# Hybrid block with product-key experts: spreading the gates with one 256-column matmul per token

## The chip, the core and the metric

One core of a Trainium2 chip runs the whole program. The metric is the device time of one execution in microseconds (us), the median of several. Engines are called PE (TensorE), DVE (VectorE), ACT (ScalarE), POOL (GpSimd) and SP (SyncE, which here only issues DMAs).

## What is computed

The program is one layer of a hybrid encoder block on 1024 tokens of width 1024: RMSNorm, an input projection, a recurrent group and an attention group, an output projection, and then the product-key expert part (PEER), followed by a last RMSNorm. The change lies in the expert part, cut here to what matters:

```python
# h: 1024 tokens x 1024; experts: 128 x 128 = 16384 single neurons; 8 heads x 16 picks = 128 picks a token
experts = (e1 * 128 + e2).reshape(t, 128)
gates = jax.nn.softmax(top_s, axis=-1).reshape(t, 128)
pre = jnp.einsum('td,tkd->tk', xb, u_tab[eb])
act = jax.nn.gelu(pre) * gb
y = jnp.einsum('tk,tkd->td', act, v_tab[eb])
```

## The kernel before

The expert part has three functions: `score` (queries, scores and picks), `experts_up` (activations) and `experts_down` (the second table). The change touches only `experts_up`, lines 1114 to 1485.

`experts_up` handles the 1024 tokens in two ways. Three tiles of 128 tokens are handled **by rows**: for each token and pick POOL fetches the expert's row of `u` with an indirect DMA (`fetch`, L1349) and DVE takes its dot product with the token (`dot`, L1453), 384 dots in all. The other 640 tokens are handled **densely**: all 16384 activations are computed by PE, and the gates are spread over all 16384 experts, mostly as zeros, so that `experts_down` can multiply the two.

The dense products run over 128 chunks `c` of the table, each 128 experts x 1024. SP loads a chunk (`load`, L1213), ACT rounds it to the high part `uT_hi` (`high`, L1287), DVE subtracts to get the low part `uT_lo` (`low`, L1436; POOL does it for the first 24 chunks, L1340), PE multiplies in three terms, 24 matmuls of 320 columns for each half of the tokens (`multiply`, L1251), ACT applies the gelu (`gelu`, L1301), and SP stores the activations (L1221).

The gates are spread by one-hot vectors, 4 tokens at a time; the 640 tokens are 160 such groups `g`. For each token two 128 x 128 matrices are made: `first_hot` (which of the 128 first keys each pick has) and the one of the second key, scaled by the gate. To keep the precision of fp32 with matmuls in float32r, the gate is split into a high and a low part. DVE makes the one-hots of a group (`hot_group`, L1446 and L1447), ACT scales them into `second_hot_lo` and `second_hot_hi` (`gate`, L1309 and L1312), PE multiplies `first_hot` with the high and with the low part into the same PSUM columns (`spread_out`, two 128-column matmuls per token, L1241 and L1243), and ACT copies the 512 sums to SBUF, 32 tokens innermost (`spread_out` of ACT, L1294). This copy writes one element per 128 bytes:

```python
A(spread[:, part % 2, :, col * GROUP:(col + 1) * GROUP].rearrange("p e t -> p t e"),
  spread_ps[:, g % 2], ACT.Copy).then_inc(spread_read, 1)
```

Eight groups make a part of 32 tokens, 2 MB, which SP stores to DRAM (L1227), 20 parts in all.

The order of the work is written out by hand. Every engine goes through the same count `q` of quarters, four for each chunk, 512 in all, with 12 dense matmuls in each; its instructions stand in that order and it never turns back. `groups_at(q)` lists the groups that PE spreads and ACT copies in quarter `q`: 160 groups over the quarters 84 to 496, one in 2.575 quarters. DVE makes the one-hots of a group five quarters earlier, ACT scales them four quarters earlier, `low(c + 1)` stands at the second quarter of chunk `c` (DVE q = 4c + 1), `high(c + 1)` at its first (ACT q = 4c), and the dots are spread over the quarters 58 to 508. Seven steps that turn picks into keys (`key`, L1400 to L1409) come in for each of the eight tiles of tokens.

The waits that tie the engines: `high(c)` waits for its load and for PE to be done with chunk c - 2; `low(c)` waits for `high(c)`; PE starts chunk c after `low(c)`. SP's queue is in order too: load of chunk c + 2, store of the activations of chunk c (which waits for both gelus), then the store of a part of gates if its last group lies in that chunk (which waits for `spread_read`), then the next load. A load that follows a store of gates therefore stands behind it.

Of the kernel before, what the change touches and what calls it, by code (L numbers as in the profile page):

```python
# [1113 lines left out]
def experts_up(nc, d, m, sem):  # L1114
# [22 lines left out]
    KEY_STEPS, TURN_AFTER = 7, 12  # L1137

# [21 lines left out]
    with ExitStack() as own_memory:  # L1160
# [7 lines left out]
        second_hi = sb("second_hot_hi", [P, SLOTS, GROUP, NK], F32R)  # L1168
        second_lo = sb("second_hot_lo", [P, SLOTS, GROUP, NK], F32R)
# [9 lines left out]
        pre = ps("expert_pre", [P, 4, HALF])  # L1179
        spread_ps = ps("spread_ps", [P, 2, GROUP, NK])  # L1180
# [7 lines left out]
        spread_done, spread_read = sem("spread_done"), sem("spread_read")  # L1188
# [18 lines left out]
        with nc.Block() as block:  # L1207
# [27 lines left out]
            def _(pe):  # L1235
                def spread_out(g):
                    pe.wait_ge(gates_hot, g + 1)
                    if g >= 2:
                        pe.wait_ge(spread_read, g - 1)
                    for j in range(GROUP):  # L1240
                        nc.tensor.matmul(spread_ps[:, g % 2, j], first_hot[:, g % SLOTS, j],  # L1241
                                         second_hi[:, g % SLOTS, j], start=True, stop=False)
                        last = nc.tensor.matmul(spread_ps[:, g % 2, j], first_hot[:, g % SLOTS, j],  # L1243
                                                second_lo[:, g % SLOTS, j], start=False, stop=True)
                    last.then_inc(spread_done, 1)
# [3 lines left out]
                def multiply(c, half, n):  # L1249
                    part, t, k = terms[n]  # L1250
                    last = nc.tensor.matmul(pre[:, (2 * c + half) % 4, 0:WIDTH], part[:, c % 2, k],  # L1251
# [13 lines left out]
                for q in range(QUARTERS):  # L1265
# [3 lines left out]
                    if q % 2 == 0 and 2 * c + half >= 4:  # L1269
                        pe.wait_ge(act_done, 2 * c + half - 3)  # L1270
# [9 lines left out]
            def _(act):  # L1280
# [8 lines left out]
                def spread_out(g):  # L1289
                    part, col = divmod(g, PART)  # L1290
                    act.wait_ge(spread_done, g + 1)
                    if col == 0 and part >= 2:
                        act.wait_ge(spread_stored[part % 2], 16 * (part // 2))
                    A(spread[:, part % 2, :, col * GROUP:(col + 1) * GROUP].rearrange("p e t -> p t e"),  # L1294
                      spread_ps[:, g % 2], ACT.Copy).then_inc(spread_read, 1)

                def gelu(c, half):
                    act.wait_ge(pre_done, 2 * c + half + 1)
                    if half == 0 and c >= 2:
                        act.wait_ge(act_stored[c % 2], 16 * (c // 2))  # L1300
                    A(act_out[:, c % 2, half * WIDTH:(half + 1) * WIDTH], pre[:, (2 * c + half) % 4, 0:WIDTH],  # L1301
                      ACT.Gelu_apprx_tanh).then_inc(act_done, 1)
# [61 lines left out]
            def _(dve):  # L1364
# [84 lines left out]

                def dot(k):  # L1450
# [6 lines left out]
                for q in range(KEYS_FROM, QUARTERS + 4):  # L1457
# [11 lines left out]
                    for n in range(3):  # L1469
                        for t in tiles_at(q, TURN_AFTER + 2 + n):  # L1470
                            if t >= F:
                                keep(t, n)
                    for g in hots_at(q):
# [372 lines left out]
```

## Time and profile before

| | us |
|---|---|
| median of 3 runs | 3349.49 (3339.14 to 3357.92) |
| the profiled execution | 3346.13 |
| its span in the profile | 3344.3 |
| PE busy | 2998.9 (90% of the span) |
| DVE busy | 2380.4 (71%) |
| ACT busy | 1255.3 (38%) |
| POOL busy | 1306.6 (39%) |
| first and last copy of a group (L1294) start at | 1328.8 and 2235.5 |
| first and last gelu (L1301) start at | 1151.8 and 2270.7 |

The profile is of one execution. Busy time counts an engine's instructions, whatever they achieve; matmuls overlap one another, so a matmul's duration is longer than the distance from one to the next. A group of instructions is given with its line, its engine, its operation, the names of what it writes and reads, its count, and the idle time of its engine just before it with what ended that idle time. The stretch from 1316 to 2236 us is the one in which groups of gates are spread, and the text calls it the stretch.

### The profile page before, as it was taken

What the parts mean: (1) busy time and instruction counts of PE and PEld (TensorE: products, weight loads), DVE (VectorE), ACT (ScalarE), POOL (GpSimd) and SP (SyncE); (2) the same over time, 40 slices, a digit from 0 to 9 for tenths busy, and PEclk for the clock granted to TensorE, in tenths of its full rate; (3) what the DMA queues carried; (4) which work ended last, traced back from release to release, by engine and by line L of the source; (5) the groups of instructions that cost most, each with busy time, mean ns of one, the idle gap of its engine ahead of it and who ended that gap; (6) DMA issues with size and microseconds to landing.
All of it is one profiled execution on the core that took longest, in us unless ns stands there. A gap on an engine that the chain in (4) does not pass through costs nothing. (4 is left out here: it accounts for less than half of the span.)

```text
span 3344.3 us, 41495 instructions
## 1 busy us (share of the span) xinstructions
PE 2998.9 (90%) x15103; PEld 2493.3 (75%) x15103; DVE 2380.4 (71%) x4578; ACT 1255.3 (38%) x2579; POOL 1306.6 (39%) x1087
## 2 busy tenths in 40 slices
PE   7999999988699897999999999991998999998996
PEld 3347576753499897998999999991876777777775
DVE  1083133222279589988798888874999999999997
ACT  2141223221111223777778778761222222222221
POOL 1000100000158557555445555543445545445543
PEclk9999556569899998999999999995999999999998
DMA  3000000021211147899999989997999999999996
GB/s 136 0 25 26 0 1 1 0 85 50 63 39 39 40 136 258 325 348 327 357 336 335 361 318 361 360 359 274 366 355 329 349 355 346 352 348 345 352 349 217
DMA packets 303079, 754.55 MB, mean 226 GB/s; under 512 B 22736, under 2 KB 127184, under 8 KB 300320
## 3 DMA queue, kind: packets, MB, share of 16 engines
q0 software_dynamic: 111072, 403.02, 33.0%
q1 hardware_dynamic: 190752, 344.76, 29.2%
q10 hardware_dynamic: 1056, 4.19, 0.3%
q8 instruction: 116, 1.90, 0.2%
q14 instruction: 83, 0.68, 0.1%
HBM read 659.61 MB, written 92.27 MB: 225 GB/s over the span
## 5 line engine op out<-in xcount | busy, mean ns | idle before, releaser
L1251 PE MATMUL expert_pre<-h2T,uT_hi 128*128 128x320 f32 x4096 | 681.7, 316 | 61.5 <-DVE uT_lo L1436 33.4
L1546 POOL DMA_INDIRECT v_rows<-in_peer_v,row_numbers x384 | 515.6, 1343 | 546.6 <-DVE y L1611 458.5
L1349 POOL DMA_INDIRECT u_rows<-in_peer_u,row_numbers x384 | 537.0, 1399 | 440.8 <-DVE row_weights L1453 383.7
L1251 PEld LDWEIGHTS expert_pre<-h2T,uT_hi 128*128 128x128 f32 x4096 | 623.5, 192 | 66.3 <-DVE uT_lo L1436 36.7
L1650 PE MATMUL expert_out<-v_hi,w_hi 128*128 128x512 f32 x1280 | 511.7, 400 | 145.4 <-DVE w_lo L1589 145.3
L1611 DVE SCALAR_TENSOR_TENSOR y<-v_rows,row_weights,y 128x1024 f32<-128x1024 f32 x384 | 487.0, 1277 | 52.7 <-DMA v_rows<-in_peer_v,row_numbers 36.0
L1650 PE MATMUL expert_out<-v_lo,w_hi 128*128 128x512 f32 x1280 | 507.7, 397 | 0.0
L1650 PE MATMUL expert_out<-v_hi,w_lo 128*128 128x512 f32 x1280 | 506.3, 396 | 0.0
L1453 DVE CUSTOM_DVE_ANT_0 u_rows<-u_rows,h_rows_kept 128x1024 f32<-128x1024 f32 x384 | 464.8, 1237 | 5.7 <-DMA u_rows<-in_peer_u,row_numbers 5.7
L1650 PEld LDWEIGHTS expert_out<-v_hi,w_hi 128*128 128x128 f32 x1280 | 246.1, 192 | 209.6 <-DVE w_lo L1589 158.3
L1570 ACT ACTIVATE w_hi<-acts_times_gates 128x640 fp32r<-128x640 f32 x128 | 94.8, 741 | 750.8 <-DVE acts_times_gates L1582 750.8
L1251 PE MATMUL expert_pre<-h2T,uT_lo 128*128 128x320 f32 x2048 | 344.9, 310 | 0.0
L1251 PEld LDWEIGHTS expert_pre<-h2T,uT_lo 128*128 128x128 f32 x2048 | 314.7, 190 | 0.0
L1650 PEld LDWEIGHTS expert_out<-v_hi,w_lo 128*128 128x128 f32 x1280 | 245.9, 192 | 52.8
L1650 PEld LDWEIGHTS expert_out<-v_lo,w_hi 128*128 128x128 f32 x1280 | 246.1, 192 | 50.8
L1309 ACT ACTIVATE second_hot_lo<-second_hot_hi,gateT_lo 128x128 fp32r<-128x128 f32 x640 | 203.4, 393 | 68.7 <-DVE second_hot_hi L1447 68.6
L1436 DVE TENSOR_TENSOR uT_lo<-u_chunk,uT_hi 128x1024 fp32r<-128x1024 f32 x104 | 127.1, 1222 | 143.0 <-ACT uT_hi L1287 141.9
L1603 DVE TENSOR_TENSOR y<-y,expert_out 128x512 f32<-128x512 f32 x320 | 216.9, 678 | 7.3 <-PE expert_out L1650 7.1
L1312 ACT ACTIVATE second_hot_hi<-second_hot_hi,gateT_hi 128x128 fp32r<-128x128 f32 x640 | 203.4, 392 | 0.0
L1294 ACT ACTIVATE pick_memory<-spread_ps 128x512 f32<-128x512 f32 x160 | 180.7, 1129 | 20.9 <-PE spread_ps L1243 20.7
L1301 ACT ACTIVATE expert_acts<-expert_pre 128x320 f32<-128x320 f32 x256 | 112.3, 439 | 184.3 <-PE expert_pre L1251 183.6
L1018 POOL CAST wq_hi<-wq_tile 128x1024 fp32r<-128x1024 f32 x16 | 16.6, 1040 | 403.9 <-DMA wq_tile<-in_peer_wq 358.7
(260 smaller groups left out, 4432.5 us busy)
## 6 DMA issues: line engine op xcount, KB each, us to landing
u_chunk<-in_peer_u_turned SPq DMA_DIRECT2D x128, 512.0 KB, 6.9
v_chunk<-in_peer_v SPq DMA_DIRECT2D x128, 512.0 KB, 6.7
acts_dram<-expert_acts SPq DMA_DIRECT2D x128, 320.0 KB, 4.9
gates_dram<-pick_memory SPq DMA_DIRECT2D x20, 2048.0 KB, 10.9
acts_times_gates<-acts_dram SPq DMA_DIRECT2D x128, 320.0 KB, 8.2
gates_group<-gates_dram SPq DMA_DIRECT2D x32, 1280.0 KB, 15.9
wq_tile<-in_peer_wq SPq DMA_DIRECT2D x16, 512.0 KB, 4.0
w_qkv<-in_w_in SPq DMA_DIRECT2D x6, 1024.0 KB, 5.1
```

Of the source, the lines that this page charges most:

```text
L1251: last = nc.tensor.matmul(pre[:, (2 * c + half) % 4, 0:WIDTH], part[:, c % 2, k], m.h2T[:, t, k, HALVES[half]], start=n == 0, stop=n == le ...
L1294: A(spread[:, part % 2, :, col * GROUP:(col + 1) * GROUP].rearrange("p e t -> p t e"), spread_ps[:, g % 2], ACT.Copy).then_inc(spread_read, 1)
L1301: A(act_out[:, c % 2, half * WIDTH:(half + 1) * WIDTH], pre[:, (2 * c + half) % 4, 0:WIDTH], ACT.Gelu_apprx_tanh).then_inc(act_done, 1)
L1309: A(second_lo[:, g % SLOTS, j], second_hi[:, g % SLOTS, j].bitcast(F32), ACT.Identity, scale=gate_lo[:, t % 2, first + j:first + j + 1])
L1312: last = A(second_hi[:, g % SLOTS, j], second_hi[:, g % SLOTS, j].bitcast(F32), ACT.Identity, scale=gate_hi[:, t % 2, first + j:first + j ...
L1349: pool.indirect_dma_start(rows[:, k % RING], None, d.peer_u, bass.IndirectOffsetOnAxis(ap=m.row_of[:, f, slot:slot + 1], axis=0)).then_inc ...
L1436: v.tensor_tensor(ulo[:, c % 2], u[:, c % 2], uhi[:, c % 2].bitcast(F32), ALU.subtract).then_inc(ulo_dve, 1)
L1453: v.tensor_tensor_reduce(out=rows[:, k % RING], in0=rows[:, k % RING], in1=m.h2_kept[:, f], scale=1.0, scalar=0.0, op0=ALU.mult, op1=ALU.a ...
L1546: pool.indirect_dma_start(rows[:, k % ROW_RING], None, d.peer_v, bass.IndirectOffsetOnAxis(ap=m.row_of[:, f, slot:slot + 1], axis=0)).then ...
L1603: v.tensor_tensor(m.y[:, F + t, cols], m.y[:, F + t, cols], out[:, bank % RING], ALU.add).then_inc(out_read, 1)
L1611: v.scalar_tensor_tensor(out=m.y[:, f], in0=rows[:, k % ROW_RING], scalar=m.row_weight[:, f, slot:slot + 1], in1=m.y[:, f], op0=ALU.mult, ...
L1650: last = nc.tensor.matmul(out[:, bank % RING], a[:, n % 2, c, tokens], e[:, n % 2, c, cols], start=k == 0, stop=k == len(terms) - 1)
```

## The change

Three things change, all in `experts_up`.

The high and low second hot matrices lie side by side in one buffer, and PE multiplies `first_hot` with both at once: one matmul of 256 columns per token in place of two of 128 columns. The two products land in separate PSUM columns, so a group takes two PSUM banks, two groups four.

ACT copies the high half to SBUF as before (512 elements, one per 128 bytes) and signals `spread_hi_read`. A new DVE instruction, `add_low_gates`, adds the low half from PSUM to what ACT wrote, in place, with the same strided pattern, and it now gives `spread_read`. It stands two quarters after the group's own quarter (`ADD_AFTER = 2`), ahead of the one-hots and dots of that quarter.

`expert_pre`, the PSUM ring of the dense products, has three banks in place of four (`PRE = 3`): PE waits for the gelu of three halves ago, not four.

```diff
@@ -1135,6 +1135,7 @@
     DOTS_FROM, DOTS_TO = 58, QUARTERS - 4
     LEAD = SLOTS - 1
     KEY_STEPS, TURN_AFTER = 7, 12
+    PRE, ADD_AFTER = 3, 2
 
     def paced(q, total, first, stop):
 
@@ -1165,8 +1166,8 @@
         ulo = sb("uT_lo", [P, 2, KT, P], F32R)
         act_out = sb("expert_acts", [P, 2, DENSE])
         first_hot = sb("first_hot", [P, SLOTS, GROUP, NK], F32R)
-        second_hi = sb("second_hot_hi", [P, SLOTS, GROUP, NK], F32R)
-        second_lo = sb("second_hot_lo", [P, SLOTS, GROUP, NK], F32R)
+        second = sb("second_hot_hi_lo", [P, SLOTS, GROUP, 2, NK], F32R)
+        second_hi, second_lo = second[:, :, :, 0], second[:, :, :, 1]
         spread = m.pick_memory[:, 0:2 * NK * 32].rearrange("p (b e t) -> p b e t", b=2, t=32)
         hot = m.pick_memory[:, 2 * NK * 32:2 * NK * 32 + PH * TOP * TOP].rearrange("p (k r) -> p k r", r=TOP)
         route = sb("route", [P, 2, 3, PH, TOP])
@@ -1176,8 +1177,8 @@
         rows = sb("u_rows", [P, RING, D])
         dots = m.row_weight
         below_top = rows[:, 0].rearrange("p (h t k) -> p h t k", h=PH, k=TOP)
-        pre = ps("expert_pre", [P, 4, HALF])
-        spread_ps = ps("spread_ps", [P, 2, GROUP, NK])
+        pre = ps("expert_pre", [P, PRE, HALF])
+        spread_ps = ps("spread_ps", [P, 2, GROUP, 2, NK])
         route_ps = ps("route_ps", [P, 3, P])
 
         u_in = [sem("u_in0"), sem("u_in1")]
@@ -1185,7 +1186,7 @@
         pre_done, act_done = sem("pre_done"), sem("expert_act_done")
         act_stored = [sem("act_stored0"), sem("act_stored1")]
         hot_done, gates_hot = sem("hot_done"), sem("gates_hot")
-        spread_done, spread_read = sem("spread_done"), sem("spread_read")
+        spread_done, spread_hi_read, spread_read = sem("spread_done"), sem("spread_hi_read"), sem("spread_read")
         spread_stored = [sem("spread_stored0"), sem("spread_stored1")]
         picked, decoding, decoded = sem("late_heads_picked"), sem("late_decode_step"), sem("late_heads_decoded")
         gating, shifted, exp_done = sem("gate_step"), sem("pairs_shifted"), sem("pairs_exp")
@@ -1238,17 +1239,15 @@
                     if g >= 2:
                         pe.wait_ge(spread_read, g - 1)
                     for j in range(GROUP):
-                        nc.tensor.matmul(spread_ps[:, g % 2, j], first_hot[:, g % SLOTS, j],
-                                         second_hi[:, g % SLOTS, j], start=True, stop=False)
                         last = nc.tensor.matmul(spread_ps[:, g % 2, j], first_hot[:, g % SLOTS, j],
-                                                second_lo[:, g % SLOTS, j], start=False, stop=True)
+                                                second[:, g % SLOTS, j], start=True, stop=True)
                     last.then_inc(spread_done, 1)
 
                 terms = [(part, t, k) for part, t in ((uhi, 0), (uhi, 1), (ulo, 0)) for k in range(KT)]
 
                 def multiply(c, half, n):
                     part, t, k = terms[n]
-                    last = nc.tensor.matmul(pre[:, (2 * c + half) % 4, 0:WIDTH], part[:, c % 2, k],
+                    last = nc.tensor.matmul(pre[:, (2 * c + half) % PRE, 0:WIDTH], part[:, c % 2, k],
                                             m.h2T[:, t, k, HALVES[half]], start=n == 0, stop=n == len(terms) - 1)
                     if n == len(terms) - 1:
                         last.then_inc(pre_done, 1)
@@ -1266,8 +1265,8 @@
                     c, half, first = q // 4, q % 4 // 2, q % 2 * len(terms) // 2
                     if q % 4 == 0:
                         wait_low(pe, c)
-                    if q % 2 == 0 and 2 * c + half >= 4:
-                        pe.wait_ge(act_done, 2 * c + half - 3)
+                    if q % 2 == 0 and 2 * c + half >= PRE:
+                        pe.wait_ge(act_done, 2 * c + half - PRE + 1)
                     for n in range(first, first + len(terms) // 2):
                         multiply(c, half, n)
                     for g in groups_at(q):
@@ -1292,13 +1291,13 @@
                     if col == 0 and part >= 2:
                         act.wait_ge(spread_stored[part % 2], 16 * (part // 2))
                     A(spread[:, part % 2, :, col * GROUP:(col + 1) * GROUP].rearrange("p e t -> p t e"),
-                      spread_ps[:, g % 2], ACT.Copy).then_inc(spread_read, 1)
+                      spread_ps[:, g % 2, :, 0], ACT.Copy).then_inc(spread_hi_read, 1)
 
                 def gelu(c, half):
                     act.wait_ge(pre_done, 2 * c + half + 1)
                     if half == 0 and c >= 2:
                         act.wait_ge(act_stored[c % 2], 16 * (c // 2))
-                    A(act_out[:, c % 2, half * WIDTH:(half + 1) * WIDTH], pre[:, (2 * c + half) % 4, 0:WIDTH],
+                    A(act_out[:, c % 2, half * WIDTH:(half + 1) * WIDTH], pre[:, (2 * c + half) % PRE, 0:WIDTH],
                       ACT.Gelu_apprx_tanh).then_inc(act_done, 1)
 
                 high(0)
@@ -1447,6 +1446,12 @@
                     v.tensor_tensor(second_hi[:, g % SLOTS], keys, each(routeT[:, i % 2, 1, tokens]), ALU.is_equal
                                     ).then_inc(hot_done, 1)
 
+                def add_low_gates(g):
+                    part, col = divmod(g, PART)
+                    to = spread[:, part % 2, :, col * GROUP:(col + 1) * GROUP].rearrange("p e t -> p t e")
+                    dve.wait_ge(spread_hi_read, g + 1)
+                    v.tensor_tensor(to, to, spread_ps[:, g % 2, :, 1], ALU.add).then_inc(spread_read, 1)
+
                 def dot(k):
                     f, slot = divmod(k, P)
                     dve.wait_ge(fetched[k % RING], 16 * (k // RING + 1))
@@ -1470,6 +1475,8 @@
                         for t in tiles_at(q, TURN_AFTER + 2 + n):
                             if t >= F:
                                 keep(t, n)
+                    for g in groups_at(q - ADD_AFTER):
+                        add_low_gates(g)
                     for g in hots_at(q):
                         hot_group(g)
                     for k in dots_at(q):
```

On DVE, between two low parts (`uT_lo`, those of the chunks 62 and 63; `u_rows` are the dots, `pick_memory` the SBUF buffer of the spread gates). Before:

```order
L1436 TENSOR_TENSOR uT_lo<-u_chunk,uT_hi 128x1024 [waits u_hi_done]
L1453 ISA u_rows,row_weights<-u_rows,h_rows_kept 128x1024 [waits u_row_in3]
L1453 ISA row_weights 128x1
L1446 TENSOR_TENSOR first_hot<-iota,routeT 128x512 [waits spread_done,routeT_done]
L1447 TENSOR_TENSOR second_hot_hi<-iota,routeT 128x512
L1453 ISA u_rows,row_weights<-u_rows,h_rows_kept 128x1024 [waits u_row_in4]
L1453 ISA row_weights 128x1
L1453 ISA u_rows,row_weights<-u_rows,h_rows_kept 128x1024 [waits u_row_in5]
L1453 ISA row_weights 128x1
L1446 TENSOR_TENSOR first_hot<-iota,routeT 128x512 [waits spread_done]
L1447 TENSOR_TENSOR second_hot_hi<-iota,routeT 128x512
L1436 TENSOR_TENSOR uT_lo<-u_chunk,uT_hi 128x1024 [waits u_hi_done]
```

The first part of the same place after the change:

```order
L1435 TENSOR_TENSOR uT_lo<-u_chunk,uT_hi 128x1024 [waits u_hi_done]
L1453 TENSOR_TENSOR pick_memory<-pick_memory,spread_ps 128x4x128 [waits spread_hi_read]
L1458 ISA u_rows,row_weights<-u_rows,h_rows_kept 128x1024 [waits u_row_in3]
L1458 ISA row_weights 128x1
L1445 TENSOR_TENSOR first_hot<-iota,routeT 128x512 [waits spread_done,routeT_done]
L1446 TENSOR_TENSOR second_hot_hi_lo<-iota,routeT 128x4x128
L1458 ISA u_rows,row_weights<-u_rows,h_rows_kept 128x1024 [waits u_row_in4]
L1458 ISA row_weights 128x1
L1458 ISA u_rows,row_weights<-u_rows,h_rows_kept 128x1024 [waits u_row_in5]
L1458 ISA row_weights 128x1
L1453 TENSOR_TENSOR pick_memory<-pick_memory,spread_ps 128x4x128 [waits spread_hi_read]
```

Nothing is taken from DVE; two additions (L1453 of the changed kernel) stand among what was there, each behind a wait for ACT's copy.

On PE, the first quarter of a chunk with a group in it. Before:

```order
L1251 MATMUL expert_pre<-h2T,uT_hi 128x320 [waits expert_act_done,u_lo_by_dve]
L1251 MATMUL expert_pre<-h2T,uT_hi 128x320 x11
L1241 MATMUL spread_ps<-second_hot_hi,first_hot 128x128 [waits spread_read,gates_hot]
L1243 MATMUL spread_ps<-second_hot_lo,first_hot 128x128
L1241 MATMUL spread_ps<-second_hot_hi,first_hot 128x128
L1243 MATMUL spread_ps<-second_hot_lo,first_hot 128x128
L1241 MATMUL spread_ps<-second_hot_hi,first_hot 128x128
L1243 MATMUL spread_ps<-second_hot_lo,first_hot 128x128
L1241 MATMUL spread_ps<-second_hot_hi,first_hot 128x128
L1243 MATMUL spread_ps<-second_hot_lo,first_hot 128x128
L1251 MATMUL expert_pre<-h2T,uT_hi 128x320 x4
```

After:

```order
L1250 MATMUL expert_pre<-h2T,uT_lo 128x320 x8
L1250 MATMUL expert_pre<-h2T,uT_hi 128x320 [waits expert_act_done,u_lo_by_dve]
L1250 MATMUL expert_pre<-h2T,uT_hi 128x320 x11
L1242 MATMUL spread_ps<-second_hot_hi_lo,first_hot 128x256 [waits spread_read,gates_hot]
L1242 MATMUL spread_ps<-second_hot_hi_lo,first_hot 128x256 x3
L1250 MATMUL expert_pre<-h2T,uT_hi 128x320 x4
```

Eight matmuls of a group became four of twice the width, at the same place.

## Rows read from the trace of the kernel before

**Rows 1.** The page's slices of the whole span, 40 of 83.6 us.
```profile
PE   7999999988699897999999999991998999998996
...
DVE  1083133222279589988798888874999999999997
...
PEclk9999556569899998999999999995999999999998
```

**Rows 2.** The stretch: us, busy time (instructions) of each engine, PEclk, DMA share, GB/s.
```profile
1316.00:2236.00 920.00, 889.83 (x6285) 886.56 (x6284) 787.06 (x1175) 714.45 (x1754) 499.68 (x361) 0.98 0.93 344
```

**Rows 3.** Who waited in that stretch: total us, times, longest us.
```profile
DVE uT_lo L1436 <- ACT uT_hi L1287: 130.2, 47, 7.6
...
PE expert_pre L1251 <- DVE uT_lo L1436: 29.1, 12, 6.4
...
ACT uT_hi L1287 <- DMA u_chunk<-in_peer_u_turned: 78.5, 22, 6.7
```

**Rows 4.** PE's weight loads in order of time: start, length, line, count.
```profile
1601.49 0.19 PEld L1241 LDWEIGHTS spread_ps<-second_hot_hi,first_hot 128*128 128x128 f32 x1
...
1602.42 2.36 PEld L1251 LDWEIGHTS expert_pre<-h2T,uT_hi 128*128 128x128 f32 x16
1604.73 1.21 PEld L1251 LDWEIGHTS expert_pre<-h2T,uT_lo 128*128 128x128 f32 x8
```

**Rows 5.** DVE's groups in 1316 to 2236 us: busy us, mean ns, idle before.
```profile
L1453 DVE CUSTOM_DVE_ANT_0 u_rows<-u_rows,h_rows_kept 128x1024 f32<-128x1024 f32 x356 | 427.3, 1227 | 4.9 <-DMA u_rows<-in_peer_u,row_numbers 4.8
L1436 DVE TENSOR_TENSOR uT_lo<-u_chunk,uT_hi 128x1024 fp32r<-128x1024 f32 x101 | 123.5, 1222 | 131.3 <-ACT uT_hi L1287 130.2
```

**Rows 6.** DVE in order of time.
```profile
1602.29 0.69 DVE L1446 TENSOR_TENSOR first_hot<-iota,routeT 128x512 fp32r<-128x512 f32 x1
1602.90 0.69 DVE L1447 TENSOR_TENSOR second_hot_hi<-iota,routeT 128x512 fp32r<-128x512 f32 x1
1603.50 1.24 DVE L1453 CUSTOM_DVE_ANT_0 u_rows<-u_rows,h_rows_kept 128x1024 f32<-128x1024 f32 x1
```

**Rows 7.** Three lines by themselves: duration ns min/median/max.
```profile
L1294 ACT ACTIVATE pick_memory<-spread_ps x160: 1046/1132/1195, 1328.8 to 2235.5; 128x512 f32<-128x512 f32 x160
...
L404 ACT ACTIVATE qT_kT<-product x16: 578/597/599, 166.4 to 283.0; 128x512 f32<-128x512 f32 x16
...
L1603 DVE TENSOR_TENSOR y<-y,expert_out x320: 667/678/689, 2345.6 to 3319.6; 128x512 f32<-128x512 f32 x160
```

**Rows 8.** SP, ACT, DVE and PE around one store of gates, in order of time.
```profile
1603.96 0.32 SPq L1227 DMA_DIRECT2D gates_dram<-pick_memory  x1
1604.32 0.49 SPq L1213 DMA_DIRECT2D u_chunk<-in_peer_u_turned  x1
...
1618.05 1.06 ACT L1287 ACTIVATE uT_hi<-u_chunk 128x1024 fp32r<-128x1024 f32 x1 [4.61 <-DMA u_chunk<-in_peer_u_turned]
...
1604.82 1.23 DVE L1436 TENSOR_TENSOR uT_lo<-u_chunk,uT_hi 128x1024 fp32r<-128x1024 f32 x1
...
1619.15 1.23 DVE L1436 TENSOR_TENSOR uT_lo<-u_chunk,uT_hi 128x1024 fp32r<-128x1024 f32 x1 [5.88 <-ACT uT_hi L1287]
...
1620.42 2.61 PE L1251 MATMUL expert_pre<-h2T,uT_hi 128*128 128x320 f32 x16 [1.02 <-DVE uT_lo L1436]
```

**Rows 9.** Two other stores of gates and the low part behind each.
```profile
2148.04 0.43 SPq L1227 DMA_DIRECT2D gates_dram<-pick_memory  x1
...
2164.46 1.23 DVE L1436 TENSOR_TENSOR uT_lo<-u_chunk,uT_hi 128x1024 fp32r<-128x1024 f32 x1 [6.42 <-ACT uT_hi L1287]
...
2194.30 0.32 SPq L1227 DMA_DIRECT2D gates_dram<-pick_memory  x1
...
2207.17 1.23 DVE L1436 TENSOR_TENSOR uT_lo<-u_chunk,uT_hi 128x1024 fp32r<-128x1024 f32 x1 [4.94 <-ACT uT_hi L1287]
```

**Rows 10.** DMA issues of the stretch: KB each, median us to landing.
```profile
u_chunk<-in_peer_u_turned SPq DMA_DIRECT2D x104, 512.0 KB, 7.4
gates_dram<-pick_memory SPq DMA_DIRECT2D x19, 2048.0 KB, 10.9
```

## The prediction

> **What bounds the kernel now.** I read the page first, then the stretch, then its waits, then the order of time around one store of gates.
>
> The page's slices show PE at 9 in most of the second half, and DVE at 8 and 9 beside it [rows 1]. The change touches only the slices 16 to 27, the stretch from 1316 to 2236 us. There PE is busy for 889.8 of 920 us and DVE for 787.1, ACT for 714.5 [rows 2]. So PE is the bound, with a granted clock of 0.98, nearly all of it on the upper of its levels, 2.4 GHz. DVE has 133 us to spare, and what the reader must see is where they lie: 130.2 of them end with ACT's high part of a chunk, in 47 waits of up to 7.6 us, all of them ahead of the 1.22 us of `uT_lo` [rows 3, 5]. PE in turn lost 29.1 us to DVE's low part [rows 3], and ACT waited 78.5 us for the chunk's load [rows 3].
>
> The order of time shows why. SP issues the store of a part of gates at 1603.96 and the next load right behind it, at 1604.32. The load is late, ACT can make the high part only at 1618.05 after 4.61 us of waiting, DVE the low part at 1619.15 after 5.88 us of idling, and PE starts the chunk at 1620.42 after 1.02 us [rows 8]. A load lands after 7.4 us in the median, a store of gates after 10.9 [rows 10], and they follow each other. From the store's issue to the start of that low part it is 15.2 us here, 16.4 and 12.9 in the longest and shortest case [rows 9], 15.0 on average over the 16 of the 20 parts in which ACT waited for that load. So DVE's spare time isn't spread evenly: most of it is a chain of two transfers behind each store of gates.
>
> **PE's part.** Eight 128-column matmuls take from 1601.49 to 1602.42, 0.93 us a group [rows 4]. The 320-column ones follow each other by 2.31 / 16 = 0.144 us [rows 4]. A 256-column matmul isn't in the stretch: it costs no less than 0.93 / 8 = 0.116 and no more than 0.144. I take 0.135, nearer the wider one, so 0.54 a group. PE loses 160 x 0.39 = 62 us of work and comes to about 828 us (bounds 815 to 833 with the same sum).
>
> **DVE's part, the term that decides.** 160 additions of 512 elements come in. Where nothing strides, an addition of 512 elements with one operand in PSUM takes 678 ns [rows 7]. Instructions follow each other a little faster than their duration: 0.61 and 0.60 us for 0.69 [rows 6]. So the cheap end is 0.60 us, or 96 us in all. But the new addition reads and writes SBUF at one element per 128 bytes. The one row with that pattern is ACT's copy, 1132 ns, where a contiguous copy of 512 from PSUM takes 597 [rows 7]: the stride costs 535 ns, 1.05 ns an element. If DVE pays it once, reads and writes going on side by side, the addition takes 1.21 us and 1.13 from one to the next: 181 us in all. If it pays twice it is 1.67, or 267 us. I take 1.13, since it is the pattern itself that was measured, and keep 0.60 and 1.67 as ends.
>
> The Trainium skill bears on this from both sides. "VectorE: DVE Perf Modes" (the section on the TRN2 errata) gives an fp32 addition of N elements (N + 151) / 0.96 ns, 691 ns for 512, with no word of a stride; by that the sum would be the cheap end below. The contiguous 678 ns agree. "Advanced Engine Details and Errata" (Memory Cachelines) says that SBUF works at full speed only when at least two accesses fall on one 16-byte line; that speaks against this change, and ACT's 1132 against 597 ns agree.
>
> **The new sum for DVE.** With 181 us more, DVE has 787 + 181 = 968 us of work, against 828 on PE and about 715 on ACT. DVE becomes the bound. Its idle time doesn't go away altogether, since the chain behind each store remains, and it begins later: `spread_read` now comes from DVE's addition, two quarters on. If the part's last group lies in quarter 4c + r, SP can issue the store when DVE has passed 4c + r + 2, and DVE reaches `low(c + 3)`, whose load stands behind the store, at 4c + 9. That leaves 7 - r quarters; the 20 last groups fall evenly on r = 0 to 3. A quarter of DVE's work lasts 968 / 412 = 2.35 us, so 16.4, 14.1, 11.7 or 9.4 us for a chain of 15.0. DVE idles 0, 0.9, 3.3 or 5.6 us, 2.4 on average, 20 times: 49 us. (With PE ahead, the gelus that the store waits for are done before the addition.) The stretch becomes 968 + 49 = 1017 us, 97 more than now.
>
> **What costs nothing.** ACT's copy has as many elements as before. The third bank instead of the fourth: PE waits for a gelu of three halves ago, over 3 us after that half ended, and the gelu stands one quarter on in ACT's order; with ACT late by the 4.61 us above it stands behind the high part of a chunk further on, not of this one. If that cover were gone, PE's slack of 140 us would pay for it. PE's wait for the addition of two groups before: it lies three quarters back in DVE's order, and PE has slack as well. Behind the waiting addition on DVE stand one-hots and dots; ACT's copy that it waits for was made two quarters earlier, so I count no wait. POOL's fetches wait for the dots and just slow down with DVE.
>
> **Sum.** The profiled execution took 3346, so 3346 + 97 = 3443 us. It lies 3 us under the median of the runs, which I leave in the range.
>
> **The rivals.**
>
> *The cheap addition, with the chain* (0.60 us). DVE has 883 us of work, a quarter is 2.14 us, the chain's 15.0 us meet 15.0, 12.9, 10.7 or 8.6: 3.2 us of idling, 64 in all. The stretch is 947, the time 3373. For it speaks the contiguous row, against it ACT's strided row.
>
> *Faster: the additions fill DVE's waits.* If the addition is cheap and all of it falls into the time that DVE now idles, the stretch is DVE's work alone, 883 us against 920, and the time is 3309; with 10 us of leftovers 3319. PE's 828 allow it. The place is the 5.88 us ahead of `low` [rows 8]: it decides whether the store is issued as early as now. It needs DVE's work and remaining idling under 903 us, so an addition under 0.7 us and at most 1 us of waiting per part. Against it: the store now waits for DVE.
>
> *The dear one.* The addition at 1.67 us: 1054 us of work, a quarter of 2.56, idling of 35 us, together 1089, the time 3515. Or the addition at 1.13 but the waits stay whole: 968 + 131 = 1099, the time 3525.
>
> *The 256-column matmul saves nothing* (0.23 us instead of two of 0.116). PE would stay at 890 us and still be under DVE's 968; the forecast holds, and only the fast rival falls.
>
> **How the numbers follow.** About 0.5%, or 17 us, is what a measurement of this kernel can tell from no change. My forecast, one stride paid, spreads from 3400 to 3480 with the waits: 0.58. Cheap with the chain: 0.14, from 3350 to 3390, a third of it within 17 us. Fast: 0.11. Dear: 0.17. The range from 3360 to 3515 leaves out the fast rival and a little at the top. Slower by over 0.5%: 0.83; within: 0.06; faster: 0.11.
>
> **What would show it.** In the profile after, the new addition at about 1.2 us each (0.68 would make it the cheap case, 1.75 the dear one); DVE busy for some 95% of a stretch of about 1017 us; PE busy for clearly less, with waits for `uT_lo` of well over 100 us instead of 29; DVE's waits for the high part down from 130 to about 50; the weight loads of the spread matmuls 0.13 us apart; waits of PE for gelus near none. The prediction is wrong if PE is still the bound, or if DVE idles over 100 us.

## The result, and the profile after

| | before | after |
|---|---|---|
| median, us | 3344.31 (4 runs, 3337.86 to 3357.92) | 3440.69 (4 runs, 3439.07 to 3447.98) |
| ratio of the times | | 1.0287, 95% interval 1.0248 to 1.0325 |
| span of the profiled execution | 3344.3 | 3446.2 |
| first to last copy of a group by ACT | 1328.8 to 2235.5, 906.7 | 1336.6 to 2340.4, 1003.8 |

The change makes the kernel 2.9% slower, by 96 us. The stretch in which gates are spread grew by 97.1 us in the profile; the remaining 5 us between the two spans lie outside it, 8 us ahead of it and 3 the other way behind it. The 8 us arise before the expert part: its first gelu starts at 1151.8 us before and at 1159.9 after, and from there to the first copy it is 177 us in both. Medians and ratios, here and below, leave out one execution (3498.16 us, run e7), which fell into the chip's slower state.

The stretch after the change, 1017 us from 1324 to 2341 (the columns are as in [rows 2]):

```profile
1324.00:2341.00 1017.00, 868.50 (x5639) 848.59 (x5637) 953.80 (x1327) 711.29 (x1754) 602.64 (x357) 0.94 0.86 310
```

DVE is busy for 953.8 of 1017 us, 94%, and PE for 868.5, 85%: they have changed places. The traffic fell from 344 to 310 GB/s, since all is slower.

Who waits now in that stretch, the answers for DVE, PE and ACT one below the other (they answer to [rows 3]):

```profile
DVE uT_lo L1435 <- ACT uT_hi L1286: 31.4, 10, 6.0
DVE u_rows L1458 <- DMA u_rows<-in_peer_u,row_numbers: 29.5, 10, 6.7
...
PE expert_pre L1250 <- DVE uT_lo L1435: 129.3, 61, 8.9
PE spread_ps L1242 <- DVE pick_memory L1453: 17.5, 8, 5.9
...
ACT second_hot_hi_lo L1308 <- DVE second_hot_hi_lo L1446: 220.3, 110, 8.7
ACT uT_hi L1286 <- DMA u_chunk<-in_peer_u_turned: 72.8, 17, 9.1
```

PE's waits for the low part grew from 29.1 to 129.3 us, DVE's waits for the high part fell from 130.2 to 31.4, and ACT now waits mostly for DVE's one-hots (220.3 us against 68.6). Everybody waits for DVE.

The new instruction, and the three lines that answer to [rows 7] and [rows 4]:

```profile
L1453 DVE TENSOR_TENSOR pick_memory<-pick_memory,spread_ps x160: 1135/1234/1339, 1340.9 to 2346.8; 128x512 f32<-128x512 f32 x160
...
L1293 ACT ACTIVATE pick_memory<-spread_ps x160: 1005/1110/1180, 1336.6 to 2340.4; 128x512 f32<-128x512 f32 x160
```

```profile
1619.07 0.57 PEld L1242 LDWEIGHTS spread_ps<-second_hot_hi_lo,first_hot 128*128 128x128 f32 x4
1619.57 2.37 PEld L1250 LDWEIGHTS expert_pre<-h2T,uT_hi 128*128 128x128 f32 x16
```

The addition takes 1.23 us, nearly twice the 0.68 of one that doesn't stride [rows 7]. The four matmuls of a group take 0.50 us, 0.125 each.

One store of gates in order of time, SP first, then ACT, DVE and PE (it answers to [rows 8]):

```profile
1935.72 0.32 SPq L1222 DMA_DIRECT2D acts_dram<-expert_acts  x1
1943.28 0.32 SPq L1228 DMA_DIRECT2D gates_dram<-pick_memory  x1
1943.64 0.43 SPq L1214 DMA_DIRECT2D u_chunk<-in_peer_u_turned  x1
...
1956.33 1.06 ACT L1286 ACTIVATE uT_hi<-u_chunk 128x1024 fp32r<-128x1024 f32 x1 [9.07 <-DMA u_chunk<-in_peer_u_turned]
...
1941.99 1.26 DVE L1453 TENSOR_TENSOR pick_memory<-pick_memory,spread_ps 128x512 f32<-128x512 f32 x1
...
1957.42 1.22 DVE L1435 TENSOR_TENSOR uT_lo<-u_chunk,uT_hi 128x1024 fp32r<-128x1024 f32 x1 [6.02 <-ACT uT_hi L1286]
...
1958.70 3.56 PE L1250 MATMUL expert_pre<-h2T,uT_hi 128*128 128x320 f32 x12 [7.65 <-DVE uT_lo L1435]
```

SP had stored the chunk's activations at 1935.72 and then stood until DVE's addition ended at 1943.25; the store and the load behind it went out at once. The load held ACT up by 9.07 us, DVE by 6.02 and PE by 7.65. Of the 19 stores in the stretch 15 were issued 0.03 us after the end of their part's last addition, the other 4 within 0.9 us of it. After this pause PE's first 12 matmuls took 3.56 us; 12 such took 1.92 at 1946.88, when PE had been working. The view by windows has the granted clock (third number from the right) before the pause, behind it, and 3.6 us on:

```profile
1945.00:1951.00 6.00, 6.00 (x43) 5.78 (x41) 6.00 (x10) 2.27 (x8) 5.08 (x4) 1.00 0.99 407
1958.70:1962.30 3.60, 3.60 (x13) 3.60 (x14) 3.60 (x6) 3.60 (x11) 1.15 (x1) 0.50 0.58 234
1962.30:1966.00 3.70, 3.70 (x25) 3.70 (x25) 3.70 (x6) 3.70 (x11) 1.16 (x2) 0.88 0.79 204
```

It went from 2.4 to 1.2 GHz and back. Over the stretch it is 0.94 where it was 0.98 [rows 2]. PE isn't the bound here, so this should cost little; no run isolates it.

### The profile page after: what moved, and what is told of

It reads as the page before. It is cut to its first block and busy times, and to the rows that moved or that the text cites. A ratio compares the mean times of both kernels' runs of the same rounds, so it can differ in the third digit from the quotient of the medians.

```text
span 3446.2 us, 40375 instructions
## 1 busy us (share of the span) xinstructions
PE 2986.9 (87%) x14463; PEld 2462.2 (71%) x14463; DVE 2554.3 (74%) x4738; ACT 1253.2 (36%) x2579; POOL 1418.7 (41%) x1087
## 5 line engine op out<-in xcount | busy, mean ns | idle before, releaser
L1250 PE MATMUL expert_pre<-h2T,uT_hi 128*128 128x320 f32 x4096 | 705.3, 324 | 165.9 <-DVE uT_lo L1435 138.7
L1348 POOL DMA_INDIRECT u_rows<-in_peer_u,row_numbers x384 | 645.9, 1682 | 433.2 <-DVE row_weights L1458 370.1
L1250 PEld LDWEIGHTS expert_pre<-h2T,uT_hi 128*128 128x128 f32 x4096 | 646.3, 199 | 185.0 <-DVE uT_lo L1435 155.7
L1308 ACT ACTIVATE second_hot_hi_lo<-second_hot_hi_lo,gateT_lo 128x128 fp32r<-128x128 f32 x640 | 204.8, 392 | 220.8 <-DVE second_hot_hi_lo L1446 220.3
L1311 ACT ACTIVATE second_hot_hi_lo<-second_hot_hi_lo,gateT_hi 128x128 fp32r<-128x128 f32 x640 | 202.9, 389 | 0.0
L1453 DVE TENSOR_TENSOR pick_memory<-pick_memory,spread_ps 128x512 f32<-128x512 f32 x160 | 197.0, 1231 | 0.0
L1293 ACT ACTIVATE pick_memory<-spread_ps 128x512 f32<-128x512 f32 x160 | 176.5, 1103 | 0.2
```

The lines of the kernel that those rows point to most:

```text
L1250: last = nc.tensor.matmul(pre[:, (2 * c + half) % PRE, 0:WIDTH], part[:, c % 2, k], m.h2T[:, t, k, HALVES[half]], start=n == 0, stop=n == ...
L1308: A(second_lo[:, g % SLOTS, j], second_hi[:, g % SLOTS, j].bitcast(F32), ACT.Identity, scale=gate_lo[:, t % 2, first + j:first + j + 1])
L1311: last = A(second_hi[:, g % SLOTS, j], second_hi[:, g % SLOTS, j].bitcast(F32), ACT.Identity, scale=gate_hi[:, t % 2, first + j:first + j ...
L1348: pool.indirect_dma_start(rows[:, k % RING], None, d.peer_u, bass.IndirectOffsetOnAxis(ap=m.row_of[:, f, slot:slot + 1], axis=0)).then_inc ...
L1453: v.tensor_tensor(to, to, spread_ps[:, g % 2, :, 1], ALU.add).then_inc(spread_read, 1)
```

## The experiments

Theory A is the prediction's: DVE's sum of work sets the pace, the stride is half of the addition's price, and the chain of gates store, load, high part and low part adds idling of its own. The rivals put the loss elsewhere: in the ring of three banks or PSUM, or in the transfers whatever their order; and some runs ask whether the place of the addition counts. The ratios are with runs of the kernel before on the same chip.

| run | median, us | ratio to before, 95% | stretch, first to last copy |
|---|---|---|---|
| the change | 3440.69 | 1.0287 (1.0248 to 1.0325) | 1003.8 |
| e1_high_only | 3326.35 | 0.9961 (0.9922 to 1.0000) | 886.7 |
| e2_contiguous_add | 3381.54 | 1.0110 (1.0038 to 1.0181) | 938.6 |
| e3_strided_read | 3421.61 | 1.0246 (1.0167 to 1.0325) | 979.0 |
| e4_strided_write | 3414.04 | 1.0226 (1.0139 to 1.0313) | 970.6 |
| e5_load_first_after | 3406.08 | 1.0174 (1.0122 to 1.0225) | 961.5 |
| e6_load_first_before | 3328.44 | 0.9941 (0.9913 to 0.9968) | 893.0 |
| e7_add_a_quarter_later | 3447.94 (3 runs) | 1.0391 (1.0302 to 1.0481) | 1034.2 |
| e8_three_banks_before | 3349.02 | 1.0003 (0.9979 to 1.0028) | 902.1 |
| e9_high_only_load_first | 3292.32 | 0.9840 (0.9772 to 0.9908) | 856.1 |
| e10_pool_low_104 | 3470.08 | 1.0395 (1.0331 to 1.0460) | 1022.4 |
| e11_pool_low_64 | 3434.55 | 1.0277 (1.0216 to 1.0338) | 990.5 |
| e12_add_a_quarter_earlier | 3431.79 | 1.0263 (1.0194 to 1.0332) | 983.4 |

The ratios are those on record, which aren't quite the quotients of the medians. They are furthest apart in e7, where 3447.94 over the 3345.33 of its kernel before is only 1.031. The last column is of one profiled execution each. It leaves out what happens ahead of the change, and that differs by more than some of the effects: in e7 the first gelu starts at 1124.7 us and in the change at 1159.9, though the code ahead of it is the same, and from 600 to 900 us the granted clock was 0.85 in e7 and 0.74 in the change.

### PE's part alone, and the banks alone

```diff
-                      spread_ps[:, g % 2, :, 0], ACT.Copy).then_inc(spread_hi_read, 1)
+                      spread_ps[:, g % 2, :, 0], ACT.Copy).then_inc(spread_read, 1)
...
-                    for g in groups_at(q - ADD_AFTER):
-                        add_low_gates(g)
```

> The changed kernel without DVE's additions: ACT's copy gives spread_read itself, and the low half of the gates is left out of the output. It has the 256-column matmuls, the ring of three banks and nothing else. Theory A (the loss is the 197 us of additions on DVE, and the later store of gates): PE is the bound again with 160 x 0.43 us less work (0.50 us a group against 0.93), about 821 us, and the waits of the chain behind the stores, 30 to 50 us; the stretch is 850 to 870 us against 920 and the time 3275 to 3300. Rival B (the loss lies in the ring of three banks or in the four banks of the spread sums): still over 3400. Rival C (PE's saving was never worth anything, because the chain of store, load and high part sets the pace): 3335 to 3350.

Measured: 3326.35 us. Without the additions 114 us of the change's time are gone, and it is level with the kernel before or a little faster (the interval ends at 1.0000). Rival B falls. But the time isn't 3275 to 3300, and it lies under rival C's range as well: of PE's saved work little reaches the end. The waits show where it went:

```profile
1328.00:2228.00 900.00, 835.48 (x5640) 828.99 (x5639) 780.13 (x1171) 708.82 (x1753) 504.73 (x360) 0.97 0.93 350
...
DVE uT_lo L1435 <- ACT uT_hi L1286: 112.5, 41, 7.9
...
PE expert_pre L1250 <- DVE uT_lo L1435: 61.2, 21, 7.5
```

PE is busy for 54 us less than in [rows 2] and waits 32 us more for the low part than in [rows 3]. That would fit a chain behind the stores with a length of its own. Run e9 below tests this. DVE's busy time here, 780.1 us, is also the cleanest base for the additions: 953.8 - 780.1 = 173.7 us, 1.09 us each.

For the banks, the kernel before with three in place of four:

```diff
-        pre = ps("expert_pre", [P, 4, HALF])
+        pre = ps("expert_pre", [P, 3, HALF])
...
-                    if q % 2 == 0 and 2 * c + half >= 4:
-                        pe.wait_ge(act_done, 2 * c + half - 3)
+                    if q % 2 == 0 and 2 * c + half >= 3:
+                        pe.wait_ge(act_done, 2 * c + half - 2)
```

> The kernel before with three banks for the dense products instead of four. Theory A: PE waits for no gelu, since that of three halves ago is long done: 3340 to 3350, no change. Rival B (the ring of three banks is a part of the loss): 3370 or more.

Measured: 3349.02 us, ratio 1.0003 (0.9979 to 1.0028), and no wait of PE for a gelu. So the kernel before runs as well on three banks as on four, and the change has no such wait either.

### The price of the stride

The addition's two SBUF sides are made contiguous, both (e2), the write (e3, which still reads with the stride) and the read (e4, which still writes with it). The edit of e2; e3 and e4 replace only one of the two:

```diff
+        apart = sb("sums_apart", [P, 2, GROUP, NK])
...
-                    v.tensor_tensor(to, to, spread_ps[:, g % 2, :, 1], ALU.add).then_inc(spread_read, 1)
+                    if g >= 2:
+                        dve.wait_ge(spread_read, g - 1)
+                    v.tensor_tensor(apart[:, g % 2], keys, spread_ps[:, g % 2, :, 1], ALU.add).then_inc(spread_read, 1)
```

> The addition's SBUF sides no longer stride: it adds the low half to the key numbers, in rows of 128, and writes into two blocks of its own, so the low half of the gates is left out of the output; count, PSUM side, place in the order and the waits stay (with one more, for its own addition of two groups before, long done). Theory A: 0.68 us each and 0.60 from one to the next; DVE has about 875 us of work and idles some 60 us in the stretch, time 3360 to 3390. If the additions fill DVE's waits instead: 3300 to 3330. Rival B (not the stride): 3430 to 3450.

> Only the reading of the addition strides: it reads the spread gates at one element per 128 bytes and writes rows of 128 into two blocks of its own (the low half of the gates is left out of the output). If reads and writes go side by side and each alone costs the whole stride: 1.2 us each, time 3430 to 3450, and the same for the writing alone. If each pays its half: about 0.95 us each, 3395 to 3415. If only the write pays: 0.68 us and 3360 to 3390.

> Only the writing of the addition strides: it adds the low half to the key numbers, read in rows of 128, and writes into the spread gates as the change does (so the gates in the output are wrong numbers). If each side alone costs the whole stride: 1.2 us each, time 3430 to 3450. If each pays its half: 0.95 us, 3395 to 3415. If only the read pays: 0.68 us, 3360 to 3390. ACT's copy, which only writes with the stride, speaks for the write.

Measured, the line of the addition in e2, e3 and e4 (duration ns min/median/max):

```profile
L1456 DVE TENSOR_TENSOR sums_apart<-iota,spread_ps x160: 672/682/702, 1344.4 to 2282.7; 128x512 f32<-128x512 f32 x160
```

```profile
L1456 DVE TENSOR_TENSOR sums_apart<-pick_memory,spread_ps x160: 990/1103/1159, 1343.0 to 2323.2; 128x512 f32<-128x512 f32 x160
```

```profile
L1453 DVE TENSOR_TENSOR pick_memory<-iota,spread_ps x160: 1004/1105/1157, 1321.8 to 2294.4; 128x512 f32<-128x512 f32 x160
```

None strides: 682 ns. One side strides, whichever: 1103 and 1105, 422 ns more. Both: 1234, only 130 more than one. So the price is about that of one stride, as if the two sides went on side by side, as the prediction took it; a half each (0.95 us) and the double price (1.75) are both wrong, and a whole stride from each side alone (1.2) is too. The durations decide this, not the times: e4's 3414.04 us lies in the range given for the half price and e3's 3421.61 in none, and the intervals of e3, e4 and the change overlap. From e2 to the change the stretch grew by 65 us for 160 x 0.55 = 88 us of longer additions; DVE's idling took up the rest. Its waits ahead of the low part were 31.4 us in the change and 75.0 in e2:

```profile
1328.00:2280.00 952.00, 852.40 (x5641) 840.80 (x5640) 872.31 (x1331) 710.92 (x1753) 476.09 (x360) 0.95 0.91 332
...
DVE uT_lo L1436 <- ACT uT_hi L1287: 75.0, 23, 8.9
```

Even with the cheap addition the change is 1.1% slower than before (interval 1.0038 to 1.0181), though DVE's 872 us of work are less than the 920 that the stretch took before. The prediction's first rival said 3373 us for such an addition, and 3381.54 came; the fast one (3309 to 3319) isn't reached.

### The chain behind the stores of gates

SP's queue issues the load of the next chunk ahead of the store of gates:

```diff
+                def store_gates(c):
+                    for q in range(4 * c, 4 * c + 4):
...
                 for c in range(NK):
                     if c + 2 < NK:
                         load(c + 2)
+                    if c:
+                        store_gates(c - 1)
                     sp.wait_ge(act_done, 2 * c + 2)
                     sp.dma_start(d.acts[c], act_out[:, c % 2]).then_inc(act_stored[c % 2], 16)
-                    for q in range(4 * c, 4 * c + 4):
```

> The changed kernel with one move in SP's queue: the store of a part of gates stands behind the next chunk's load instead of ahead of it. Nothing else changes. Theory A: in the changed kernel DVE idles 31 us ahead of uT_lo behind the stores, and the load no longer waits for the addition; most of the 31 us goes, the DMA waits of the dots (30 us) stay: 3405 to 3425. Rival (the load's lateness comes from the total of traffic, not from the order): 3435 to 3450.

> The kernel before with the same move in SP's queue. Theory A: PE's 29 us of waits for uT_lo go for the most part, DVE's and ACT's waits change their place but PE stays the bound: 3315 to 3330. Rival (traffic, not order): 3340 to 3350.

> e1 (no addition on DVE, low half of the gates left out of the output) with the load ahead of the store of gates, as in e5. Theory A (in e1 PE's 67 us of saved matmuls were given back as waits for uT_lo, 63 us against 29, because the chain behind the stores of gates has a length of its own): the waits fall to about 25 us and the stretch to 850 us, 40 less than e1; time 3280 to 3295. Rival (PE's waits come from DVE's own order or from traffic): 3315 to 3330 as in e1.

Measured: 3406.08, 3328.44 and 3292.32 us, all three in theory A's ranges. The waits in the three stretches, of DVE and at the end of PE:

```profile
DVE uT_lo L1439 <- ACT uT_hi L1290: 1.5, 3, 0.9
```

```profile
DVE uT_lo L1440 <- ACT uT_hi L1291: 101.1, 55, 4.5
```

```profile
DVE u_rows L1462 <- DMA u_rows<-in_peer_u,row_numbers: 50.7, 41, 4.1
DVE uT_lo L1439 <- ACT uT_hi L1290: 33.0, 29, 2.8
...
PE expert_pre L1254 <- DVE uT_lo L1439: 40.1, 17, 8.5
```

In the change (e5) DVE's waits for the high part go from 31.4 to 1.5 us. In the kernel before (e6) PE is the bound, so DVE still waits, but no longer for more than 4.5 us at once; PE's waits fell from 29.1 to 19.2 us and the time by 0.6%. And e9 against e1 is one move of one transfer and 34 us, 3292 against 3326 (the low half of the gates is left out in both); DVE's waits for the high part fall from 112.5 to 33.0. So PE's saving is real, and a part of it was held back by the order of two DMAs. Not all of it comes through: against e6, the kernel before with the same order, e9 is 36 us faster, where PE has 69 us less to do. PE still waits 40.1 us for the low part, not the 25 that were expected.

The move does two things at once: the load no longer stands behind SP's wait for the last group of the part, and the 2 MB of gates no longer go ahead of it. No run separates the two.

The place of the addition, with `PRE, ADD_AFTER = 3, 2` made `3, 3` (e7) and `3, 1` (e12):

> The changed kernel with the addition three quarters behind its group in place of two. Theory A: DVE's work is the same, but the store of gates is issued a quarter (2.35 us) later, so the chain of 15 us has 6 - r quarters instead of 7 - r to hide in: DVE idles about 20 x 1.6 us more, and PE waits more for the addition; 3460 to 3485. Rival (the store's place in DVE's order doesn't count, DVE's sum of work does): 3435 to 3450.

> The changed kernel with the addition one quarter behind its group in place of two. Theory A: the store of gates is issued a quarter (2.35 us) earlier, DVE idles less ahead of uT_lo and PE waits less for the addition: 3415 to 3435. Rival (DVE now waits for ACT's copy instead): 3440 or more, with waits of the addition for ACT in the profile.

Measured: 3447.94 and 3431.79 us, with the change's 3440.69 between them. Neither difference is clear: both intervals overlap the change's, and e7's time lies in the rival's range (3435 to 3450) and not in theory A's. What is clear is the stretch, 1034.2, 1003.8 and 983.4 us in one profile each. DVE's work is the same in the three (951.0, 953.8 and 950.9 us), so it isn't its sum alone that counts. The waits in e7 and then in e12:

```profile
DVE uT_lo L1435 <- ACT uT_hi L1286: 72.4, 18, 9.4
...
PE spread_ps L1242 <- DVE pick_memory L1453: 114.0, 66, 8.8
```

```profile
DVE uT_lo L1435 <- ACT uT_hi L1286: 29.2, 12, 5.9
...
DVE u_rows L1458 <- DMA u_rows<-in_peer_u,row_numbers: 7.1, 5, 3.1
```

A quarter later costs 41 us more idling of DVE ahead of the low part, and PE now waits 114.0 us for the addition of two groups before, where it waited 17.5. By the prediction's own sum, with a quarter less to hide the chain in, it would be 20 x 2.0 = 40 us; the 1.6 of the expectation is a slip. A quarter earlier PE's waits for the addition are 3.9 us, and DVE stands 8.2 us for ACT's copy. But there the chain doesn't follow: by the same sum DVE should idle 28 us less ahead of the low part, and it idles 29.2 instead of 31.4. What made e12's stretch shorter by 20 us is rather the rows for dots, whose late ones fell from 29.5 to 7.1 us, and no run tells why.

### Taking other work off DVE

With the load first, POOL makes the low part of more chunks: `POOL_LOWS = 24` becomes 104 (e10) or 64 (e11).

> The whole change (both halves computed) with the load ahead of the store, and POOL instead of DVE making the low part of the chunks 24 to 103. 80 x 1.15 = 92 us leave DVE, which keeps 953 - 92 = 861 us; POOL gets 80 x 2.6 = 209 us on top of 618. Theory A (DVE's sum of work is the bound): the stretch 885 to 905, the time 3325 to 3345, level with or under the kernel before. Rival (POOL, in order, is late with low parts because it waits for dots between them): over 3380.

> The same with POOL making the low parts of the chunks up to 63: 46 us leave DVE. Theory A: half of e10's gain over e5, 3360 to 3375. Rival: more than e5's 3406 if POOL is late.

Measured: 3470.08 and 3434.55 us, against e5's 3406.08. Both expectations of theory A were wrong, and by the wrong sign: e5 to e11 to e10 gets slower with each 40 chunks moved. The rival's number (over 3380) fits, and PE does wait 116.0 us for POOL's low parts in e10, but POOL's waiting for dots can't be the root, since it fell: 296.9 us in e5, 211.7 in e10. DVE itself is busy for 1029.1 us of 1036, and its busy time went up from e5's 953.5, though 92 us of work had left it:

```profile
1323.00:2359.00 1036.00, 876.42 (x5643) 854.73 (x5641) 1029.09 (x1248) 714.11 (x1754) 759.64 (x439) 0.94 0.85 305
```

Its groups in that stretch, and one moment of it, DVE and then POOL:

```profile
L1462 DVE CUSTOM_DVE_ANT_0 u_rows<-u_rows,h_rows_kept 128x1024 f32<-128x1024 f32 x354 | 525.3, 1501 | 8.8 <-DMA u_rows<-in_peer_u,row_numbers 8.8
L1457 DVE TENSOR_TENSOR pick_memory<-pick_memory,spread_ps 128x512 f32<-128x512 f32 x158 | 193.2, 1223 | 0.0
L1449 DVE TENSOR_TENSOR first_hot<-iota,routeT 128x512 fp32r<-128x512 f32 x160 | 149.8, 936 | 0.0
L1450 DVE TENSOR_TENSOR second_hot_hi_lo<-iota,routeT 128x512 fp32r<-128x512 f32 x160 | 140.0, 875 | 0.0
```

```profile
1716.04 3.25 DVE L1450 TENSOR_TENSOR second_hot_hi_lo<-iota,routeT 128x512 fp32r<-128x512 f32 x1
...
1716.32 2.40 POOL L1343 TENSOR_TENSOR uT_lo<-u_chunk,uT_hi 128x1024 fp32r<-128x1024 f32 x1
```

A one-hot that takes 0.69 us took 3.25 while POOL's subtraction of 2.40 us ran. The dots went from a mean of 1249 ns in e5 to 1501, the one-hots from 702 to about 905, and the additions, 1240 in e5, stayed at 1223. In e10's stretch 40 one-hots overlap a subtraction, and they took 2.44 us on average where the other 280 took 0.69; 39 additions overlap one and took 1.21 us against 1.23. The dots and one-hots have two inputs in SBUF, the addition one in SBUF and one in PSUM. The Trainium skill says in "SBUF — State Buffer" (section "Who interferes with whom") that an instruction of VectorE with two SBUF inputs contends with a GpSimd instruction that reads SBUF, over a port pair that "causes contention, and it's an exclusive lock", while one with at most one SBUF input outside the two-port modes isn't touched. The trace agrees, with 2.44 against 0.69 us, and the additions unchanged. The same section says that the order of issue decides who is blocked. The moment shown doesn't agree: by the records VectorE's one-hot began 0.28 us ahead of the subtraction, and it is the one that was held; but starts on POOL are rough in the profile, so this stays open.

So the work was moved to an engine that holds DVE up for longer than the work itself took on DVE: 75.6 us more in spite of 92 less, 168 in all or 2.1 us for each of the 80 subtractions of 2.5 us on POOL; each had cost DVE 1.15.

No version with both halves computed that I ran beats e6, the kernel before with the load first, at 0.9941 (0.9913 to 0.9968).

## Why the prediction was right

The forecast was 3443 us and the median is 3440.69; the stretch was to grow by 97 us, and it grew by 97.1. Taken by its own steps:

- **What bounds, and the place of DVE's waits.** Right. The waits behind the stores of gates are a chain of transfers: exchanging two DMAs takes them from 31.4 to 1.5 us in the change (e5) and from 112.5 to 33.0 in e9. In e6, where PE is the bound, 101.1 us remain in smaller pieces.
- **PE's part.** 0.135 us was taken for a 256-column matmul and 0.125 measured, so PE saves 69 us and not 62. It doesn't show in the sum, since PE isn't the bound.
- **The addition.** 1.21 us and 1.13 from one to the next were taken from ACT's strided copy; 1.23 and 1.14 are the row's (1941.99 to the one-hot at 1943.13). That it costs about one stride and not two is shown by e2 to e4: both sides together cost 552 ns, for 535 taken. The step that rested on a row of another engine held.
- **DVE's sum.** 968 us were forecast and 953.8 measured, 14 less; against e1 the additions are worth 174 us of busy time instead of 181.
- **The idling.** 49 us were forecast, all ahead of the low part. Measured were 31.4 there and 29.5 ahead of dots, for rows that came late from DRAM. The second kind I had not forecast at all; before it was 4.8 us. The two errors, 14 us less work and some 14 more idling, cancel in the 1017 us of the stretch, so its exact agreement is partly luck. The chain itself came out closer than the 31.4 suggest, since only 19 of the 20 stores lie in the stretch; behind the last one DVE idled 10.07 us more:

```profile
2362.70 1.23 DVE L1435 TENSOR_TENSOR uT_lo<-u_chunk,uT_hi 128x1024 fp32r<-128x1024 f32 x1 [10.07 <-ACT uT_hi L1286]
```

DVE's idling ahead of the low part behind each of the 20 stores adds up to 43.0 us, where 49 were forecast. By the quarter r of its chunk in which a part ends the forecast was 0, 0.9, 3.3 and 5.6 us; measured, each as the mean of five, are 0.7, 1.1, 2.7 and 4.1. The single ones scatter widely, from 0 to 10.1 us at r = 3. A later addition lengthens this idling as the chain says (e7), an earlier one hardly shortens it (e12).

- **What was to cost nothing.** The three banks did (e8), and DVE never waited for ACT's copy. PE's wait for the addition of two groups before wasn't quite nothing: 17.5 us in 8 waits, beside 129.3 for the low part, with DVE the bound anyway. With the addition a quarter later the same wait is 114.0 us, so the cover, which was called three quarters wide, was thin.
- **The rivals.** The cheap addition was tried as itself (e2) and gave 3381.5 for a forecast of 3373. The fast one doesn't come even with the cheap addition. The reason given against it fits: the waits of DVE aren't time that can be filled, since they start at a store that DVE itself now releases, and 75.0 us of them were left in e2. The cheap addition with the load first would test it and wasn't run. That the wide matmul saves nothing is excluded by its 0.125 us.

What stays open: why rows for dots came late in the change, 29.5 us. The late ones amount to 19.5 us in e5, 7.1 in e12 and 50.7 in e9, and no run isolated them.

## What to carry to other kernels

Idle time of an engine is worth nothing to added work until it is known what ends it: here 88 of the 130 us that DVE waited for the high part lay behind the 19 stores of the stretch, and an instruction that released one of these transfers moved the wait instead of filling it. Before work is given to an engine to relieve the bound, add up its work with the price of the access pattern, not of the element count, and ask which ports or queues that engine shares with the engine that it is to relieve. And where a load that the next step needs stands behind a large store in a queue, try to exchange them first: here it is the only edit that made the whole kernel faster, by 0.6%.

## What the runs showed of the hardware

- A VectorE addition of 512 elements, one operand in PSUM, takes 682 ns with contiguous SBUF sides, 1103 with one element per 128 bytes read, 1105 with the same written, 1234 with both. I had expected each side alone to cost as much as both, or half; it costs three quarters of the whole.
- A matmul in float32r follows the next after 0.116 us with 128 columns, 0.125 with 256 and 0.144 with 320, at a granted clock near the upper level: half as many matmuls of twice the width is nearly half the time (0.93 against 0.50 us a group).
- POOL's subtraction of 1024 columns held up a VectorE instruction with two SBUF inputs for about its whole length (3.25 us in place of 0.69, beside a subtraction of 2.40), and left additions with one input in PSUM as they were (1.21 us for the 39 that overlap a subtraction, 1.23 for the others).
- After a pause of 7.65 us PE's first 12 matmuls took 3.56 us in place of 1.92, at a granted clock of 0.50 in that stretch of 3.6 us and 1.00 ahead of the pause.
